# Norms of a two-block transformer: gain and split per finished tile, one factor per token behind the projection

## What is computed

```python
def rms_norm(x, g):
    return x * rsqrt(mean(x * x, axis=-1) + EPS) * g

x = x + concatenate([out_a, out_b]) @ w_out
x = x + conv_ffn(rms_norm(x, norm_ffn_g), w_up, w_conv, b_conv, w_down)
x = rms_norm(x, norm_final_g)                 # "fin": the input of the second block
# layer 0 of the second block ("a"), x and ctx share a_w_in
hx = rms_norm_2(x, norm_g[0]) * (1 + scale_x) + shift_x
hc = rms_norm_2(ctx, norm_g[0]) * (1 + scale_c) + shift_c
q, k, v, g = split(hx @ a_w_in)               # hc the same; q and k are rotated
out_x = attention(q, k, v) * silu(g)
x = x + gate_x * (out_x @ w_o[0])
# layer 1 ("b"): windowed attention, then
x = x + gate_x * (out_b @ w_o[1])
return rms_norm_2(x, final_g)                 # "out"
```

## Time and profile before

| | us |
|---|---|
| three runs: median | 3487.62 |
| lowest, highest | 3478.36, 3489.33 |
| profiled execution, whole | 3480.47 |
| its span on the core | 3478.7 |
| PE busy in it | 3012.3 (87%) |
| DVE, ACT, POOL busy | 1675.0, 923.1, 1033.4 |

### The profile page before, as it was taken

The page is one execution under the profiler, slowest core; times in us unless marked ns, Lnnn a source line. Parts: engine busy times, 40 slices in busy tenths (PEclk is TensorE's granted clock), DMA queues, the critical chain, the costliest instruction groups (busy, mean ns, idle before and its releaser), DMA issues.

```text
span 3478.7 us, 46029 instructions
## 1 busy us (share of the span) xinstructions
PE 3012.3 (87%) x16703; PEld 2575.6 (74%) x16703; DVE 1675.0 (48%) x2473; ACT 923.1 (27%) x1529; POOL 1033.4 (30%) x616
## 2 busy tenths in 40 slices
PE   3789878989999999749999898888896998888896
PEld 2678777767887888637877778887875776877785
DVE  5554243353333333464457218788725530655543
ACT  2122243121011011140001127767601101444421
POOL 2523301363544454233222212222343422000030
PEclk9899988989999999969999999999997999889997
DMA  2454322121111111003344321121010332122211
GB/s 79 160 158 139 99 54 67 36 67 42 36 60 48 36 47 56 6 18 118 127 144 153 119 107 61 70 84 54 22 49 6 121 118 91 38 55 55 68 32 52
DMA packets 223662, 256.86 MB, mean 74 GB/s; under 512 B 8953, under 2 KB 191518, under 8 KB 223534
## 3 DMA queue, kind: packets, MB, share of 16 engines
q1 hardware_dynamic: 208246, 192.56, 19.0%
q10 hardware_dynamic: 15296, 62.72, 4.6%
HBM read 188.34 MB, written 66.91 MB: 73 GB/s over the span
## 4 chain that ended last, share of the span: by engine, by line
PE 39%; DVE 5%; issue 4%; DMA 3%; ACT 2%; POOL 1%; SPq 1%; DVEq 0%; ACTq 0%; POOLq 0%
PE ps L817 7%; PE ps L818 7%; PE ps L819 7%; PE ps L966 4%; PE ps L1270 3%; PE ps L1166 3%; PE ps L1182 3%; DMA b_vt<-zb 2%; PE ps L930 1%; PE ps L882 1%; DVE w_all L2046 1%; PE ps L1246 1%; DVE mod_acc L1757 1%; PE ps L1253 1%; DVE n_t L1694 1%
## 5 line engine op out<-in xcount | busy, mean ns | idle before, releaser
L817 PE MATMUL ps<-hh,w_parts 128*128 128x512 f32 (+1 forms) x2416 | 941.6, 390 | 107.8 <-POOL hl L671 65.8
L818 PE MATMUL ps<-hl,w_parts 128*128 128x512 f32 (+1 forms) x2416 | 926.2, 383 | 0.0
L819 PE MATMUL ps<-hh,w_parts 128*128 128x512 f32 (+1 forms) x2416 | 922.8, 382 | 0.0
L817 PEld LDWEIGHTS ps<-hh,w_parts 128*128 128x128 f32 x2416 | 463.1, 192 | 220.1 <-issue 87.2
L628 POOL TENSOR_TENSOR w_parts<-w_raw,zero 128x1024 fp32r<-128x1024 f32 x132 | 268.6, 2035 | 1055.7 <-PE ps L819 736.3
L818 PEld LDWEIGHTS ps<-hl,w_parts 128*128 128x128 f32 x2416 | 463.9, 192 | 89.2 <-issue 4.8
L819 PEld LDWEIGHTS ps<-hh,w_parts 128*128 128x128 f32 x2416 | 462.3, 191 | 89.3
L630 POOL TENSOR_TENSOR w_parts<-w_raw,w_parts 128x1024 fp32r<-128x1024 f32 x132 | 317.9, 2409 | 10.4
L1979 DVE SCALAR_TENSOR_TENSOR f_y<-ps,convv,f_y 128x1023 f32<-128x1023 f32 x44 | 56.4, 1283 | 353.3 <-ACT f_y L1531 353.3
L1531 ACT ACTIVATE f_y<-ps,convv 128x1024 f32<-128x1024 f32 x44 | 53.2, 1209 | 631.5 <-PE ps L819 631.5
L2135 DVE TENSOR_SCALAR_CACHE_REDUCE b_s<-ps 128x640 f32<-128x640 f32 (+1 forms) x128 | 101.3, 791 | 242.0 <-PE ps L1253 241.6
(11 more groups left out here) (249 smaller groups left out, 5151.8 us busy)
## 6 DMA issues: line engine op xcount, KB each, us to landing
w_mod_sb<-in_w_mod SPq DMA_DIRECT2D x16, 1536.0 KB, 7.0
w_raw<-in_w_up SPq DMA_DIRECT2D x44, 512.0 KB, 3.8
w_raw<-in_a_w_in SPq DMA_DIRECT2D x32, 512.0 KB, 4.2
d_raw<-in_w_down SPq DMA_DIRECT2D x22, 512.0 KB, 5.3
w_raw<-in_w_in SPq DMA_DIRECT2D x20, 512.0 KB, 5.0
za_parts<-z_hi ACTq DMA_DIRECT2D x16, 640.0 KB, 3.0
za_parts<-z_lo ACTq DMA_DIRECT2D x16, 640.0 KB, 4.1
d_even<-za_parts SPq DMA_DIRECT2D x16, 640.0 KB, 6.9
```

The lines of the kernel that those rows point to most:

```text
L817: pe.matmul(out_, w_hi, x_hi, start=start, stop=False)
L818: pe.matmul(out_, w_hi, x_lo, start=False, stop=False)
L819: return pe.matmul(out_, w_lo, x_hi, start=False, stop=stop)
```

## The change

**ffn norm.** While w_out runs, each finished tile is multiplied by the gain (`y_g`, ACT), squared (`y_sq`), and added (`y_sum`, DVE). w_out's last tile leaves `hh` and `hl` tile by tile (`h_left`), and ACT rounds `y_g` into `hh` behind it; the low parts are made by POOL for even k and DVE for odd k. The FFN's projection takes these unscaled operands, the norm's column sums and spread stand inside it, and the row factor `f_rs` is multiplied to each up tile (`f_z`, DVE); the base and taps read `f_z`. `f_act` goes, `d_raw` has one buffer in place of two.

**ffn_down** uses three accumulators in turn and begins with the e = 0 halves of three tiles.

**fin and a norms** are one: ACT multiplies each finished residual tile by the product of both gains and the modulation (`a_gain`), rounds it, and squares the residual with `a_weight` as scale, so that the root gives the product of both factors. The shift is added by two more columns of `hh` and `hl` (their rows are TOK + 2 long), whose products are the bias of each output tile; DVE multiplies each tile of q, k, v and gates by `a_rs`, ACT adds the bias (`shift_tile`). The context rows' norm is computed inside the FFN (c_sq, c_g, c_rs). What fin does to the residual itself follows during the attention's projections: squares and sums beside q and k, the factor and gain beside the gates.

**Values** are made feature-major like the rest and turned by PE (ten transposes a tile, `turn_v`), copied by ACT and stored. The second layer's modulation has buffers of its own.

**out norm.** The residual's tiles are turned between the tiles of b_out, DVE multiplies them by the gain in a row layout (`o_rows`), and at the end the tokens' factors are multiplied to eight tiles of whole rows, four on DVE and four on ACT, which SP and ACT store.

The mix and b norms, the attentions and w_out, b projections are as before. The diff, cut to its core:

```diff
+        hh = sb("hh", [P, KT, TOK + 2], F32R)
+        hl = sb("hl", [P, KT, TOK + 2], F32R)
...
+        def even_rests(pool, name, gained, ks):
+
+            for k in ks:
+                pool.wait_ge(n_high[0], 4 * SPLITS[name] + k // 2 + 1)
+                pool.tensor_tensor(hl[:, k, X_COLS], gained(k), hh[:, k, X_COLS].bitcast(F32), ALU.subtract).then_inc(n_low[0], 1)
...
                         last.then_inc(w_used[s], 1)
+                if sums is not None and n in sums:
+                    sums[n]()
...
+        def turn_v(pe, n, s):
+
+            pe.wait_ge(z_shifted, n + 16 + 1)
+            if n == 0:
+                pe.wait_ge(r_read, R0["b_q"] + 1)
+            for part, (blocks, copied) in enumerate(((range(4), 3 * n), (range(4, 8), 3 * n - 1), (range(8, 10), 3 * n + 1))):
+                if copied > 0:
+                    pe.wait_ge(v_copied, copied)
+                for t in blocks:
+                    last = pe.transpose(bank(6 + part % 2)[:, (t - blocks.start) * P:(t - blocks.start + 1) * P],
+                                        z_out[:, s, t * P:(t + 1) * P], ident[:])
+                last.then_inc(v_turned, 1)
+
+        def project_turned(pe, name):
+
+            for n in range(8):
+                project_tile(pe, name, n // 2, n % 2, SHIFTED_SEGS)
+                if n:
+                    turn_v(pe, n - 1, (n - 1) % 2)
+                    mod_sums_within(pe, (n - 1) // 2, (n - 1) % 2, n % 2)
+
+        def project_gates(pe, name):
+
+            project_tile(pe, name, 0, 0, SHIFTED_SEGS)
+            turn_v(pe, 7, 1)
+            mod_sums_within(pe, 3, 1, 0)
+            project_tile(pe, name, 0, 1, SHIFTED_SEGS)
+            pe.wait_ge(v_copied, 24)
+            norm_columns(pe, "fin", x_sum)
+            project_tile(pe, name, 1, 0, SHIFTED_SEGS)
+            norm_spread(pe, "fin", x_t[:], SEQ, SPREAD_BANKS)
+            project_tile(pe, name, 1, 1, SHIFTED_SEGS)
+            with pe.Fori(2, 4) as i:
+                for s in range(2):
+                    project_tile(pe, name, i, s, SHIFTED_SEGS)
...
+                def down_part(m, e):
+                    wm = slice(m * P, (m + 1) * P)
+                    for c in range(0, SEQ, BANK):
+                        last = product(pe, down_acc(m)[:, c:c + BANK], d_hi[:, e, wm], d_lo[:, e, wm],
+                                       f_hi[:, e, c:c + BANK], f_lo[:, e, c:c + BANK], e == 0, e == 1)
+                    if e == 1:
+                        last.then_inc(f_down if m < KT - 1 else d_used, 1)
+
+                for s in range(2):
+                    pe.wait_ge(d_split[s], chunk + 1 + 1)
+                pe.wait_ge(f_low, 2 * chunk + 1)
+                for m in range(3):
+                    if m != 1:
+                        pe.wait_ge(acc_free[m // 2], acc_use + A0["ffn"][m // 2] + 1)
+                    down_part(m, 0)
                 pe.wait_ge(f_low, 2 * chunk + 2)
...
+                for m in range(3):
+                    down_part(m, 1)
+                for m in range(3, KT):
+                    s = (m - 3) % 2
+                    pe.wait_ge(acc_free[s], acc_use + (A0["ffn"][s] + (m - 3) // 2 + 1) + 1)
                     for e in range(2):
...
+                        down_part(m, e)
...
+            project_first(pe, "ffn", LATENT_SEGS, "ffn", lag=4, sums={
+                4: lambda: norm_columns(pe, "ffn", y_sum), 7: lambda: norm_spread(pe, "ffn", y_t[:], SEQ, SPREAD_BANKS)})
+            context_columns()
+            ffn_up(0, 1, 1, lambda: norm_spread(pe, "ctx", c_rs, CTX, SPREAD_BANKS))
+            pe.wait_ge(n_kept, NORMS["ctx"] + 1)
...
+            def turn_residual(k):
+                s = k % 2
+                pe.wait_ge(acc_free[s], A0["b_out"][s] + k // 2 + 1 + 1)
+                pe.wait_ge(out_kept[s], k // 2 + 1)
+                for t in range(QB):
+                    last = pe.transpose(bank(OUT_BANKS[s][t // 4])[:, t % 4 * P:(t % 4 + 1) * P], res[:, k, CTX + t * P:CTX + (t + 1) * P], ident[:])
+                last.then_inc(out_turned[s], 1)
+
+            for k in range(KT):
+                project_tile(pe, "b_out", k // 2, k % 2, LATENT_SEGS)
+                if k:
+                    turn_residual(k - 1)
+            turn_residual(KT - 1)
+            pe.wait_ge(n_added[0], ADDED["out"] + 4 + 1)
+            pe.wait_ge(n_added[1], ADDED["out"] + 3 + 1)
+            pe.wait_ge(n_squared[1], SQUARED["out"][1] + 4)
+            for t in range(QB):
+                blk = slice(t * P, (t + 1) * P)
+                pe.matmul(bank(0)[:, t:t + 1], o_sum[:, blk], ones[:, 0:1], start=True, stop=False)
+                last = pe.matmul(bank(0)[:, t:t + 1], o_sq[:, 1, blk], ones[:, 0:1], start=False, stop=True)
+            last.then_inc(n_summed, 1)
...
+        def square_and_gain(act, name, k):
+
+            act.wait_ge(acc_free[k % 2], A0["w_out"][k % 2] + k // 2 + 1 + 1)
+            act.wait_ge(n_added[k % 2], ADDED[name] + k // 2 + 1)
+            act.activation(y_sq[:, k % 2], res[:, k, X_COLS], ACT.Square).then_inc(n_squared[k % 2], 1)
+            act.activation(y_g[:, k], res[:, k, X_COLS], ACT.Identity, bias=zero[:], scale=vec32[:, V_FFN + k:V_FFN + k + 1]).then_inc(n_gained[k % 2], 1)
...
+        def shift_tile(act, n, s, func=ACT.Identity):
+
+            act.activation(z_out[:, s, 0:CTX], z_out[:, s, 0:CTX], func, bias=z_bias[:, s, 1:2])
+            act.activation(z_out[:, s, CTX:TOK], z_out[:, s, CTX:TOK], func, bias=z_bias[:, s, 0:1]).then_inc(z_shifted, 1)
...
+            act.wait_ge(f_low, 2 * CHUNKS)
+            for k in range(KT):
+                s = k % 2
+                act.wait_ge(acc_free[s], A0["a_qk"][s] - KT // 2 + k // 2 + 1 + 1)
+                act.wait_ge(n_low[s], 4 * SPLITS["a"] + k // 2 + 1)
+                act.activation(h_g[:, s], res[:, k, X_COLS], ACT.Identity, bias=zero[:], scale=a_gain[:, k:k + 1]).then_inc(n_gained[s], 1)
+                high_part(act, "a", k, h_g[:, s])
+                act.wait_ge(n_added[s], ADDED["a"] + k // 2 + 1)
+                act.activation(h_sq[:, s], res[:, k, X_COLS], ACT.Square, scale=a_weight[:, k:k + 1]).then_inc(n_squared[s], 1)
+            norm_sqrt(act, "a", SEQ, eps_dd)
...
+        def low_part(dve, name, k, gained):
+
+            dve.wait_ge(n_high[k % 2], 4 * SPLITS[name] + k // 2 + 1)
+            dve.tensor_tensor(hl[:, k, X_COLS], gained, hh[:, k, X_COLS].bitcast(F32), ALU.subtract).then_inc(n_low[k % 2], 1)
...
+        def scale_tile(dve, name, i, s, sums=None):
+
+            dve.wait_ge(w_used[s], i + (W0[name][s] + 1) + 1)
+            if sums is not None:
+                modulate_keep(dve, 1, *sums, acc[s][:, MOD_AT:MOD_AT + 2 * MOD_TILES])
+            dve.tensor_copy(z_bias[:, s], acc[s][:, TOK:TOK + 2])
+            dve.tensor_tensor(z_out[:, s], acc[s][:, 0:TOK], a_rs[:], ALU.mult).then_inc(acc_free[s], 1)
...
+            def ffn_taps(chunk, e, acc_use, between=None):
                 for s in range(2):
                     tile = 2 * chunk + (s * FT + e)
+                    if s == 1 and between is not None:
+                        between()
+                    dve.wait_ge(w_used[s], 2 * chunk + (W0["ffn"][s] + e + 1) + 1)
+                    if s == 1:
+                        dve.wait_ge(f_tapped[0], 4 * chunk + (2 * e + 2))
+                    elif not (isinstance(chunk, int) and chunk == 0 and e == 0):
+                        dve.wait_ge(f_tapped[1], 4 * chunk + 2 * e)
+                    dve.tensor_tensor(f_z[:], acc[s][:, 0:SEQ], f_rs[:], ALU.mult).then_inc(acc_free[s], 1)
                     dve.wait_ge(f_based[s], 2 * chunk + (e + 1))
-                    dve.scalar_tensor_tensor(f_y[:, s, 1:], acc[s][:, 0:SEQ - 1], convv[:, bass.ds(tile + 2 * FT, 1)],
+                    dve.scalar_tensor_tensor(f_y[:, s, 1:], f_z[:, 0:SEQ - 1], convv[:, bass.ds(tile + 2 * FT, 1)],
                                              f_y[:, s, 1:], ALU.mult, ALU.add).then_inc(f_tapped[s], 1)
-                    dve.wait_ge(f_tapped[s], 2 * chunk + (e + 1))
-                    dve.scalar_tensor_tensor(f_y[:, s, 2:], acc[s][:, 0:SEQ - 2], convv[:, bass.ds(tile, 1)],
-                                             f_y[:, s, 2:], ALU.mult, ALU.add).then_inc(acc_free[s], 1)
+                    dve.wait_ge(f_tapped[s], 4 * chunk + (2 * e + 1))
+                    dve.scalar_tensor_tensor(f_y[:, s, 2:], f_z[:, 0:SEQ - 2], convv[:, bass.ds(tile, 1)],
+                                             f_y[:, s, 2:], ALU.mult, ALU.add).then_inc(f_tapped[s], 1)
                 dve.wait_ge(f_gate, 2 * chunk + (e + 1))
-                dve.wait_ge(acc_free[1], acc_use + (A0["ffn"][1] + 1) + 1)
-                dve.wait_ge(f_low, 2 * chunk + e)
-                dve.tensor_tensor(f_act[:], f_g[:], f_y[:, 1], ALU.mult).then_inc(f_mult, 1)
+                dve.wait_ge(f_tapped[1], 4 * chunk + (2 * e + 2))
+                dve.tensor_tensor(f_g[:], f_g[:], f_y[:, 1], ALU.mult).then_inc(f_mult, 1)
...
```

(14 more changed lines are left out.)

731 lines of the change are left out of this document (433 added, 298 removed).

## The result

| | before | after |
|---|---|---|
| runs beside each other, median | 3488.47 us | 3400.14 us |
| lowest, highest of four | 3478.36, 3498.70 | 3389.92, 3403.24 |
| span of the profiled run | 3478.7 | 3401.4 |
| mean clock granted to PE | 0.933 | 0.946 |

The ratio is 0.974, 95% interval 0.971 to 0.978: the changed kernel is 88 us faster where 127 were forecast. 3400 lies 5 us above the range. The sign and the two largest terms were right. What failed is above all the price of the matmuls.

A forecast was written before the change was run, and what follows sets the result against it. TensorE bounds the kernel, busy 3012 of 3479 us. The terms sum to -124.3 us, taking the profiled 3480.5 to 3356; half the median's 7 us excess gives 3360. Bounds about 3335 to 3385, range extended to 3395.

The forecast's parts named there:

- the two largest terms: Merged norms ahead of the first attention, -63.4 us, and the norm in front of the FFN, -25.6 us.
- The failed step: Full-speed PE prices from the old trace: 10.9 us per tile of 48 matmuls 1024 wide, used throughout the FFN forecast.
- Rival (4): Rows of 1282 elements slow some 8000 matmuls on hh and hl; at 20 ns each, 3520 us; chance 0.03.
- FFN norm: From w_out's end to the second FFN tile pair: projection starts right behind w_out; -25.6 us, between -20 and -30.
- FFN loop: Ten FFN chunks: PE waits 1.1 us for the first residual add instead of 1.3; -2.4 us, between -11 and +4.
- fin and a norms: Last up-projection to first two attention tiles: both norms merged, done at Y+74.2 instead of Y+137.6; -63.4 us, -55 to -68.
- 14 tiles: The other attention tiles: 14.36 us plus 1.3 for the swap each, VectorE's extra load hidden; -1.1 us.
- rival (2): VectorE and GpSimd block one another; 2 us longer per attention tile gives +28, 3388 us; chance 0.10.
- Values and gates: Value and gate projections, with transposes and sums between tiles: 264.8 us instead of 277.4; -12.6 us, between -16 and 0.
- First attention: Scaling and shift behind the last gate tile delay the attention's start by +1 us.
- Last norm: Kernel's end: transposes between b_out tiles, end 22.5 us behind the last product; -20.2 us, between -24 and -11.

The follow-up runs named there:

- h3: Changed kernel with hh and hl rows of 1280 elements except in the first attention's projections, weights 128 bytes further than before; f1 rerun beside h2: 3413.0 us, ratio 0.979.
- h2: As h3 plus 128 unused bytes ahead of the weights, putting them 256 bytes further than in the kernel before: 3380.8 us, ratio 0.970.
- e1: Kernel before with hh and hl rows of 1282 elements instead of 1280, the two extra unused: 3501.83 us beside 3484.34, ratio 1.006.
- f3: Changed kernel with POOL's splits of the FFN up weights cut to 8 of 1024 columns: 3378.7 us in one run.
- g3: Changed kernel, rows of 1282 kept, with 128 bytes left free ahead of the weights (256 against before): 3398.5 us.
- f1: Changed kernel with hh and hl rows of 1280 except in the first attention's projections, context parts made behind the last up tile: 3396.4 us, ratio 0.9764.
- f4: f1 with PE's context wait moved into the first down tiles and the first value tile scaled ahead of VectorE's modulation steps: 3399.29 us, ratio 0.9764.

## Why the prediction was wrong where it was

**The failed step** is the price of a matmul taken from the trace of before and used for the kernel after ("a tile of 48 matmuls 1024 wide takes 10.9 us"). It is 11.15 in the changed kernel. Rival (4) named the cause's neighbourhood, the odd rows, but was priced only from 15 ns up, where it would turn the sign, and held at 3% with "nothing in the trace". The sign it gave, a spacing over 0.235 us, didn't come either: it was 0.232. What came was 5.7 ns. Added up over the products of before and after it makes 27.5 us, and the nearest pair of kernels, h3 and h2, differ by 32: of the 40 us between 3360 and 3400 that is most. (e1, the long rows in the kernel before, cost 17.5.) h2, at 226.7 ns, took 3380.8 us, inside the range and 21 above the forecast; some 11 of those are the values and gates and the first attention, which are off there too. A rival that can occur at any size belongs in the range at each size, not only at the one that changes the sign. It also was half the cause: rows of 1282 move the weights too. And the range was drawn tighter than its own terms: their upper bounds, simply added, reach 3402.

**FFN norm** (-25.6, measured -27.7): right. The context columns took less than 5.1, the weight wait was 1.79 where 2 was forecast. Not forecast: the 3.71 us for the context's spread and 2.3 at half speed behind it, which fall in front of the loop; without POOL's splits (f3) that wait doesn't come.

**FFN loop** (-2.4, measured +18.8): ten periods of 68.01 in place of 66.87 are +11.5, nearly all of it spacing; the wait a chunk was forecast at 1.1 and stayed at 1.3. The rest is the context wait with its slow products (6.0) and less than 2 us in the chunk ahead of the loop.

**fin and a norms** (-63.4, measured -64.6): right, step by step: f_lo at Y+10.2 (forecast 10), the last residual at Y+39.8 (39.2), both tiles at Y+73.0 (74.2).

**14 tiles** (-1.1, measured +1.1): the period is 15.79, and PE waits for nothing there but the swaps, so rival (2) is false in this place; the 0.15 a tile are spacing (from 231 to 233.5 ns a product of 512 columns).

**Values and gates** (-12.6, measured -4.5): the price of 14.36 us a tile from the earlier trace rows had the cold start of the stage in it; the steady tile was 13.92 before and is 14.07 after. By luck the turn and the sums behind a value tile were priced as much too low, 2.7 for 3.0, so that the steady period was forecast at 17.06 and came at 17.07. What was off are waits: 5.62 where 3.9 was forecast, with PE at half speed behind it and again behind one of 2.62 for weights. The two stretches around them took some 6 and 4 us more than the sum had:

```profile
1760.15 2.55 PE L937 MATMUL ps<-ident,z_out 128*128 128x128 f32 x10 [5.62 <-ACT z_out L1482]
...
1905.42 0.79 PE L858 MATMUL ps<-hh,w_parts 128*128 128x512 f32 x1 [2.62 <-POOL w_parts L671]
```

**First attention** (+1, measured +9.5): not settled. At the turn of its loop PE stands with nothing to wait for, twice:

```profile
2225.36 1.19 PE L1266 MATMUL ps<-d_even 64*128 64x512 f32 x4 [3.23 <-issue]
2228.14 3.14 PE L1266 MATMUL ps<-d_even 64*128 64x256 f32 x14 [1.59 <-issue]
```

Before there was one such stall of 1.7 us at that place. All kernels built from the changed one have the pair (2.7 to 3.3 and 1.6 to 2.6 us), all from the kernel before the one (1.6 to 2.0), and their stage takes 462.6 to 469.1 against 456.5 to 461.7. So some 3.5 us are this, with the stage's first stall (1.8 in place of 1.4), and perhaps 2 more the clock behind it, which is an estimate. The changed kernel's 469.1 is also the longest of these eleven. The trace records transfers of instructions, 16 KB each, beside these stalls: before, one from 2292.37 to 2293.47 us, ahead of the matmul that starts at 2295.15; after, two that end at 2222.70 and 2223.29 and one from 2225.76 to 2226.64. They fit a wait for instructions, but that PE waited for them isn't shown, and neither the length nor the place of the code was varied.

**Last norm** (-20.2, measured -22.5): right, at +19.9 where +22.5 was forecast; b_out with its transposes grew by 7.7 where 7.3 was, 2.1 of it spacing. (The 7.3 has all 64 transposes in it, and eight of them were counted again behind the last product, 0.9 us.)

## What to carry to other kernels

A duration read from the old trace holds for the new kernel only while the buffers that the instruction reads stay where they are: before a buffer is made longer, see what moves behind it, and afterwards compare the spacing of unchanged matmuls. Where it has changed, bringing both the row pitch and the weights back to multiples of 256 bytes is worth trying; a pad alone (g3) gave 1 of the 5.7 ns. And a wait that is removed by reordering has to be followed to the next thing that is late there: f1 paid 4.1 us in another place, and f4's new order let VectorE keep GpSimd from the next weights. Here an operation of VectorE with two SBUF inputs and one of GpSimd beside it delayed one another, so whoever moves the one has to look at the other.

## Not expected of the hardware

The spacing of products of 512 columns depends on where their operands lie: in tiles 1024 wide 226.7 ns at best, 231.1 to 233.4 when the row pitch isn't a multiple of 256 bytes or the weights don't stand at one from their place in the kernel before, at a granted clock of 1.00 in each case. In tiles over 1280 columns it is 231 ns or more in every kernel here. 128 idle bytes are worth 0.9% of the kernel (h2 against h3). VectorE and GpSimd hold one another up in both directions: a tap took 2.57 us in place of 1.28 beside a split, a split 12.28 beside modulation steps where most take 1.9. PE can stand for 3 us at the turn of a loop with nothing in the profile that it waits for. Stores in rows of 4 KB went out at 406 GB/s, those in pieces of 512 bytes, two at a time and waiting for their data, at 210.
